# Two chained transformer networks: second network's attention in 12 steps of 512 columns, its preparation between projection chunks, and 8 modulation chunks moved into a feed-forward

## The reference, cut to what matters

```python
mod = (silu(c) @ w_ada[l] + b_ada[l])                 # six vectors of 1024: shift, scale, gate, twice
h = rmsnorm(x) * (1 + scale_a) + shift_a
proj = h @ w_in                                       # 1956 columns
o_f = dense_causal_attention(q_f, k_f, v_f, F)        # fox: 4 heads of 64, with a decay F
o_m = moba_attention(q_m, k_m, v_m, t5_table)         # moba: 4 heads of 64, with a bias table
q_lat = rmsnorm(c_q) @ w_uq;  kv = rmsnorm(c_kv) @ w_ukv
o_c = dense_causal_attention([q_nope, rope(q_rot)], [k_nope, rope(k_r)], v_c)   # mla: 8 heads of 96
y = concat(rmsnorm(o_f), rmsnorm(o_m), rmsnorm(o_c)) @ w_out
x = x + gate_a * rmsnorm(y)
x = x + gate_f * rmsnorm(swiglu(rmsnorm(x) * (1 + scale_f) + shift_f))          # hidden width 2816
```

## Time and profile before

| | us |
|---|---|
| median of 3 runs (2060.04 to 2062.87) | 2060.85 |
| time of the profiled execution | 2062.21 |
| its span | 2060.4 |
| PE busy | 1817.9 (88%) |
| DVE busy | 1160.3 (56%) |
| ACT busy | 691.5 (34%) |
| mean granted clock of TensorE | 0.901 |

### The profile page before, as it was taken

How to read it: one execution, slowest core, us unless ns; L and a number is a source line. 1 busy time by engine, 2 the same in 40 slices (tenths; PEclk the granted TensorE clock), 3 DMA queues, 4 the chain that set the end, 5 groups by cost and what they waited for, 6 DMA issues and landing times.

```text
span 2060.4 us, 25840 instructions
## 1 busy us (share of the span) xinstructions
PE 1817.9 (88%) x10564; PEld 1460.7 (71%) x10564; DVE 1160.3 (56%) x1915; ACT 691.5 (34%) x883; POOL 116.5 (6%) x97
## 2 busy tenths in 40 slices
PE   5998987989999998979789979885999798859997
PEld 2775654768888887746579967444999684649996
DVE  2475455564454455654667664558665645486654
ACT  2423333241312223433343433342443233424431
POOL 1010002010000001100100000003000000030000
PEclk7998767999999999978899989887999999579999
DMA  8324455122322322344345536761564458215642
GB/s 317 122 83 164 164 205 184 41 103 82 110 94 82 121 66 95 130 164 164 113 167 181 204 131 227 273 239 50 176 198 162 154 213 298 70 49 177 198 163 89
DMA packets 172086, 310.26 MB, mean 151 GB/s; under 512 B 3232, under 2 KB 60576, under 8 KB 171328
## 3 DMA queue, kind: packets, MB, share of 16 engines
q1 hardware_dynamic: 168304, 295.03, 41.3%
q10 hardware_dynamic: 3376, 12.01, 1.7%
q0 software_dynamic: 288, 1.57, 0.2%
HBM read 306.50 MB, written 2.10 MB: 150 GB/s over the span
## 4 chain that ended last, share of the span: by engine, by line
PE 70%; DVE 17%; issue 5%; ACT 5%; DMA 2%; POOL 1%; DVEq 0%; ACTq 0%; SPq 0%; POOLq 0%
PE bank L503 52%; PE twin L503 14%; DVE arena L1059 4%; PE bank L512 4%; DVE ring_r L1059 3%; ACT arena L1689 2%; ACT arena_r L1689 2%; DMA ring<-in_w_mod 1%; DVE arena L1624 1%; DVE arena_r L1059 1%; POOL rs L1982 1%; DVE params L1059 1%; DMA ring<-in_w_in 1%; DVE params L1489 1%; DVE arena L1139 1%
## 5 line engine op out<-in xcount | busy, mean ns | idle before, releaser
L503 PE MATMUL bank<-arena_r 128*128 128x512 f32 (+2 forms) x2016 | 665.5, 374 | 4.7 <-DVE params L1505 4.4
L1059 DVE TENSOR_TENSOR ring_r<-ring,arena_r 128x4096 fp32r<-128x4096 f32 (+5 forms) x90 | 380.2, 4225 | 242.2 <-ACT arena_r L1689 242.1
L503 PEld LDWEIGHTS bank<-arena_r 128*128 128x128 f32 x2016 | 385.1, 191 | 74.1 <-DVE params L1505 5.1
L1689 ACT ACTIVATE arena_r<-ring 128x4096 fp32r<-128x4096 f32 (+5 forms) x92 | 322.6, 3507 | 339.4 <-PE bank L503 294.0
L503 PE MATMUL bank<-arena_r,actT_r 128*128 128x512 f32 (+5 forms) x768 | 267.5, 388 | 27.8 <-DVE ring_r L1059 17.4
L1689 ACT ACTIVATE arena<-bank 128x256 f32<-128x256 f32 (+6 forms) x236 | 109.0, 462 | 521.9 <-PE bank L503 411.9
L503 PE MATMUL twin<-actT_r,arena_r 128*128 128x256 f32 x1408 | 255.2, 284 | 0.5 <-DVE actT_r L1059 0.4
L503 PEld LDWEIGHTS twin<-actT_r,arena_r 128*128 128x128 f32 x1408 | 220.6, 193 | 1.0 <-DVE actT_r L1059 0.9
L503 PE MATMUL bank<-ring_r,arena_r 128*128 128x512 f32 x560 | 219.2, 391 | 0.0
L503 PE MATMUL bank<-ring_r,actT_r 128*128 128x512 f32 (+5 forms) x576 | 216.0, 375 | 0.0
L503 PE MATMUL twin<-actT_r,ring_r 128*128 128x256 f32 x704 | 199.6, 284 | 0.0
(11 more groups left out here) (165 smaller groups left out, 1804.4 us busy)
## 6 DMA issues: line engine op xcount, KB each, us to landing
ring<-in_w_mod SPq DMA_DIRECT2D x24, 2048.0 KB, 8.2
ring<-in_w_ada SPq DMA_DIRECT2D x24, 2048.0 KB, 8.0
ring<-in_w_gate_up SPq DMA_DIRECT2D x44, 1024.0 KB, 7.4
ring<-in_w_down SPq DMA_DIRECT2D x20, 2048.0 KB, 7.9
ring<-in_w_up SPq DMA_DIRECT2D x16, 2048.0 KB, 7.8
ring<-in_w_out SPq DMA_DIRECT2D x8, 2048.0 KB, 8.1
ring<-in_w_down SPq DMA_DIRECT2D x8, 1792.0 KB, 7.5
ring<-in_w_in SPq DMA_DIRECT2D x6, 2048.0 KB, 8.9
```

What stands on the lines that cost most here:

```text
L503: ins = nc.tensor.matmul(out_, lhsT, rhs, start=start, stop=stop)
L1059: return v.tensor_tensor(o, x, y, op)
L1689: return nc.scalar.activation(o, x, func, **kw)
```

## The change

1. Attention of the second network goes in 12 steps (`STEPS2`) that fill a 512-column bank: four heads of the first query tile, or two heads of the second. Scores of step j are issued beside the transposes of j-2 and the values of j-4 (`AHEAD = 4`). The values have a column of ones, so that the sum of the weights comes with them and ACT no longer accumulates.
2. The columns of `w_in_2` are reordered on the host, so that the latent columns come first. Preparation stands between the chunks: chunk 0 and 1, latent norms, chunk 2, transposes and latent products, first scores, chunk 3.
3. Group norms of fox and moba are done inside the loop, and `out2` half 0 starts with their half of the rows, before the mla norm is ready. The split of `out2` chunk 0 is wholly DVE's and stands at step 8.
4. Batch 2 of modulation (8 chunks) is multiplied in the feed-forward of layer 0 of the first network, one chunk before each first and one after each second down chunk. Batch 3 moves to the mixer of layer 1 of the first network (8 of its 12) and the second network's layer 0 (4). Its layer 1 still has 8.
5. The list of loads follows: `par2` before chunk 3 of `in2`, one modulation chunk between the halves of `out2`.

```diff
+BESIDE1 = [16, 8]
+BESIDE2 = [4, 8]
+UP_FILLS = [8, 0]
+        for q in range(4):
+            m = UP_FILLS[l] // 8
+            out += [("up1", l, 2 * q + i) for i in range(2)] + take(m)
+            out += [("down1", l, 2 * q)] + take(m) + [("down1", l, 2 * q + 1)]
+    for l in range(L):
+        ins = [("in2", l, c) for c in range(len(CH2))]
+        out += ins[:3] + [("par2", l, 0)] + ins[3:] + take(BESIDE2[l] - 1)
+        out += [("out2", l, 0)] + take(1) + [("out2", l, 1)]
+        out += [("up2", l, c) for c in range(F2 // 256)]
...
-    if key[0] == "out2" and key[2] == 0:
-        return 0
...
+STEPS2 = [(kind, part[0], part[1]) for kind in ("fox", "moba")
+          for part in (((0, 1, 2, 3), 0), ((0, 1), 1), ((2, 3), 1))]
+STEPS2 += [("mla", (0, 1, 2, 3), 0), ("mla", (4, 5, 6, 7), 0)] + [("mla", (h, h + 1), 1) for h in (0, 2, 4, 6)]
+AHEAD = 4
...
# PE, layer1, feed-forward of layer 0
+                    if l == 0:
+                        fill()
                     for half in range(2):
                         w = weights(("down1", l, 2 * q + half))
...
+                    if l == 0:
+                        fill()
...
# PE, layer2
+                for j in range(AHEAD, len(STEPS2) + AHEAD):
+                    values(j - AHEAD)
+                    if j - 2 < len(STEPS2):
+                        weights_turned(j - 2)
+                    if j < len(STEPS2):
+                        scores(j)
                         fill()
+                    if j == AHEAD:
+                        pe.wait_ge(heads_ready, nth(heads_ready))
+                        done("a", mark["kv", l])
+                    if j in (AHEAD, AHEAD + 1):
+                        for hp in (2 * (j - AHEAD), 2 * (j - AHEAD) + 1):
+                            for src, r in ((ql, "v"), (kc, "a")):
+                                turned_heads(lambda t, h: src[:, t, 96 * h:96 * h + 96], "mla", 96, hp, r)
+                    if j == 11:
+                        pe.wait_ge(mixt_ready, nth(mixt_ready))
+                        for pr in range(2):
+                            mixed_turned(0, pr, "v")
...
# DVE, layer2
+                    if j == 8:
+                        split([("out2", l, 0)])
+                    if j == 9:
+                        for at, t, c0, c1 in two:
+                            squares(sq2[:, 0:c1 - c0], mix2[:, t, c0:c1], at)
...
+                    if j == 10:
+                        group_scales(two)
```

More of the change, by code:

```diff
@@ L430, in _ @@
                         sp.wait_ge(x_ready, updates(kind, l))
+                    if kind == "par2":
+                        first = PLACE["in2", l, 0]
+                        sp.wait_ge(slot_read, sum(x not in MODS for x in order[:first + 1]))
                     w, n = (a["par1"], p1n) if kind == "par1" else (a["par2"], p2n)
@@ new lines, in layer2 @@
+                scores(0)
+                scores(1)
+                done("v", mark["in2", l, 2, 0])
+                done("a", mark["in2", l, 2, 1])
+                for hp in range(2):
+                    for at, r in ((0, "v"), (256, "a")):
+                        turned_heads(lambda t, h: qkm[:, t, at + 64 * h:at + 64 * h + 64], "moba", 64, hp, r)
+                fill()
+                project(3, 0)
+                weights_turned(0)
+                weights_turned(1)
+                scores(2)
@@ new lines, in layer2 @@
+                done("v", mark["mix2", l, 0, 1])
+                gate(L + l, 2, 0, 0)
+                w = weights(("out2", l, 0))
+                banks = [take("v") for t in range(TS)]
+                for t, (b, filled) in enumerate(banks):
+                    for i in range(4):
+                        three(b[:, :], mixed(t)(i), [x[:, i, :] for x in w], i == 0, False)
+                pe.wait_ge(mixt_ready, nth(mixt_ready))
+                for pr in range(2):
+                    mixed_turned(1, pr, "a")
@@ new lines, in layer2 @@
+                done("a", mark["mix2", l, 1, 1])
+                for t, (b, filled) in enumerate(banks):
+                    for i in range(4, KT):
+                        three(b[:, :], mixed(t)(i), [x[:, i, :] for x in w], False, i == KT - 1,
+                              filled if i == KT - 1 else None)
+                gate(L + l, 2, 0, 1)
+                w = weights(("out2", l, 1))
+                for t in range(TS):
+                    b, filled = take("v")
+                    linear(b[:, :], mixed(t), lambda i: [x[:, i, :] for x in w], filled)
@@ L1569, in layer2 @@
+                two = [(0, 0, 0, 256), (1, 1, 0, 256), (2, 0, 256, 512), (3, 1, 256, 512)]
+                third = [(4, 0, 512, 1024), (5, 1, 512, 1024)]
+                for hp in range(2):
+                    turned_heads(qfT, 66, hp)
                 for t in range(TS):
@@ new lines, in layer2 @@
+                at, t, c0, c1 = third[1]
+                squares(sq2[:, 0:c1 - c0], mix2[:, t, c0:c1], at)
+                v.tensor_scalar(ms[:, 4:6], ss[:, 4:6], 1.0 / 512, EPS, ALU.mult, ALU.add).then_inc(ms_ready, 1)
+                handed.append(("power", 4, 2))
+                group_scales(third)
+                for pr in range(2):
+                    dve.wait_ge(a_filled, mark["mix2", l, 1, pr])
+                    b = AB[(mark["mix2", l, 1, pr] - 1) % 2]
+                    rest2(1, pr, b).then_inc(a_emptied, 1)
@@ L1939, in layer2 @@
-                act.wait_ge(v_filled, mark["pv2", l])
-                split([("out2", l, 0)])
-                turned_mix((1, 3, 5, 7), S, act2_lo)
-                nth(s_filled, len(UNITS2))
-                for half in range(2):
-                    split(after(("out2", l, half)))
+                    turned_heads(kmT, 64, hp)
+                exponents2(1)
+                weights_turned(0)
+                weights_turned(1)
+                exponents2(2)
+                b = filled()
+                step(f(vfm[:, 1, :, 0:64], b[:, :].rearrange("p (h c) -> p h c", c=64), ACT.Copy), a_emptied)
@@ L1945, in layer2 @@
+                split(after(("out2", l, 0)))
+                for pr in range(2):
+                    b = filled()
+                    step(f(mix_hi2[1][:, 2 * pr:2 * pr + 2, :], b[:, :].rearrange("p (a n) -> p a n", a=2), ACT.Copy),
+                         mixh_ready)
+                split(after(("out2", l, 1)))
+                nth(s_filled, len(STEPS2))
+                nth(a_emptied, 2)
                 normed([0, 1], 2 * (L + l) + 1)
```

554 lines of the change are left out of this document (304 added, 250 removed).

## The result

The changed kernel takes 2130.5 us (2125.2 to 2131.8), the kernel before beside it 2060.4; the ratio is 1.0333 with an interval of 1.0313 to 1.0352. It is slower by 70 us. The prediction said slower, with 2097 and a range of 2060 to 2122: the direction was right, the size was not, and the time lies outside the range.

The account below looks back on a forecast made before the run. PE, busy 88% of the span, was taken as either full of products or waiting on other engines. Feed-forward +70, layer 0 -20, layer 1 -13.5 gave +36.5 on 2062.2, so 2098.7, put at 2097 for the median; range 2060 to 2122.

Parts of the forecast that it names:

- Part 1: First network's layer 0 feed-forward: modulation fills and late loads behind DVE's split cost +70 us (55 to 76).
- 4 x 9.5 + 3 x 5.85: Same feed-forward: PE stalls before tile 2, +9.5 us in four down a chunks and +5.85 in three down b chunks.
- 0.4 for the last: Last down b chunk of that feed-forward: only about 0.4 us, since the next chunk is a smaller `in1` chunk.
- down b lands at 11.3 to 11.6 after the start of down a: Feed-forward: down b's load follows B's, which has a 2 us start; PE's tile 2 then starts +9.5 us later.
- The bound of 12.1: Feed-forward: upper bound on down b's landing after down a starts, giving 10.2 us of stall each (+41).
- Sum of the feed-forward: 14.4 + 38 + 17.5 + 0.4 = +70: Layer 0 feed-forward: seven fills 14.4, down a stalls 38, three down b stalls 17.5, the last 0.4 us.
- Part 2: Behind the second network's output projection: `up2` chunk 0 loads later, +8 us per layer (5 to 9).
- Parts 3 and 4: Second network: mixer's end -19 us per layer (12 to 22); preparation gains about nothing, sum 76.3 us before 74.9.
- Part 5: Second network's attention loop: loads set its end, at 138 in layer 0 (-9 us) and 143 in layer 1 (-2.5).
- the feed-forward hides the loads: Rival for the feed-forward: loads still arrive in time and only fills cost, -19 us overall, 2042; chance 0.08.
- attention gains its full room: Rival for the second network: loops keep full clock, ending at 122 and 130, -62 us; 2054 to 2069; chance 0.15.
- its loops do not shorten: Rival for the second network: late loads and half clock hold loops at 146 to 152, giving 2114; chance 0.17.

Follow-up runs that it names:

- out2_order: Changed kernel with all modulation loads of each second-network layer put ahead of its two `out2` loads: 2112.8 us.
- loop_products_alone: Changed kernel without the eight modulation loads of the second network's layer 1, their products kept on a constant: 2110.0 us.
- early_mod: Changed kernel with one modulation load of each second-network layer put ahead of the last projection chunk's load: 2115.4 us.
- late_split: Changed kernel with DVE's split of the next chunk put behind tile 1's take-out in layer 0 feed-forward down chunks: 2052.0 us.
- late_out2_par: Changed kernel with DVE's split behind tile 1's take-out, modulation loads ahead of both `out2` loads, and `par2` ahead of the third projection chunk's load: 2045.9 us.

## Why the prediction was right in direction and wrong in size

**Part 1, the stall: the mechanism right, the size low.** Each down chunk has the wait before tile 2, released by DVE, for the reason given; moving the split removed it. The sum had 4 x 9.5 + 3 x 5.85 = 55.6 us and 0.4 for the last; the waits have 64.8 in 8 times: 11.6, 11.3, 10.5 and 10.4 in the down a chunks, 6.2, 7.8 and 6.3 in the first three down b chunks, and 0.8 in the last. The 7.8 follows an up chunk's load that took 9.4 us and not 7.8. The step that was mis-sized is "down b lands at 11.3 to 11.6 after the start of down a". It gave load B a start of 2 us; in the trace it is issued at 474.08 and down b at 474.99, a start of 0.9, and down b landed after 13.7, 13.4, 12.6 and 12.5. The bound of 12.1 was too low as well; 13.6, the row I had for two loads issued together, should have been the upper end.

**Part 1, the missing term: the clock.** "Sum of the feed-forward: 14.4 + 38 + 17.5 + 0.4 = +70" has no term for what a stall does to the products behind it. It was 20.1 us. The prediction's own rows had shown that level in attention, and it priced the attention's steps with it, but not the feed-forward. There I counted on full clock since the earlier trace rows had it; but those rows are of a round without a stall. This term is the larger part of the miss: of 97.9 - 70 = 28, 20 are clock, 7.6 the longer idle time (63.2 against 55.6), and the fills at 14.6 against 14.4 were right.

**Part 2, +8 per layer: right.** The wait of 7.78 and the split behind it ended 16.4 us after half 0 was read. The order in out2_order took it away.

**Parts 3 and 4: nearly right.** The end of the mixer in layer 0, 34.8 before, is 18.65 us (1477.63 to 1496.28), predicted 16; in layer 1 it is 17.9 (1875.21 to 1893.12). Preparation starts the loop as said: the load of the third modulation chunk is issued 76.1 and 75.8 us after the projection's start (76.3).

**Part 5: right in kind.** The loop ends at 141.2 and 142.3, predicted 138 and 143 (147.4 and 145.5 before). That the loads set this end is shown for layer 1 by loop_products_alone; for layer 0 only early_mod's 5.6 us speak for it. Layer 0 gained 14.2 (20 predicted), layer 1 12.6 (13.5).

**The rivals.** That the feed-forward hides the loads was false, and late_split shows what it takes to make it true: the rival named a landing within 2 us of the chunk's start as the point of decision, while the order of two DVE instructions decided with landings unchanged. That attention gains its full room, and that its loops do not shorten, were both false; the layers lie between. No case had the feed-forward above 76, so no case reached 2130.

## What to carry to other kernels

A split or prefetch step that waits for a load should stand behind the take-outs that PE needs next, not ahead of them; then a late load costs nothing until its own first use (late_split: the same late loads, and PE idle for 7.4 us as in the kernel before). When a ring is given more loads, price each stall twice: the wait itself and the products after it at half clock (here 63 and 20 us), and take the landing of a load behind another in the queue from the row of two together. Work that is moved from a stage bound by its loads to one bound by PE pays only after that first point is seen to, so the parts of such a change are best timed one by one.

## What the runs showed of the hardware

POOL's power of four values took 1.02 us in the earlier trace rows and 5.12 us in the changed kernel, where it starts beside DVE's split (timeline of layer 0):

```profile
1356.56 4.42 DVE L1137 TENSOR_TENSOR ring_r<-ring,arena_r 128x4096 fp32r<-128x4096 f32 x1
...
1356.73 5.12 POOL L2164 TENSOR_TENSOR rs<-ms,neghalf 128x4 f32<-128x4 f32 x1 [18.42 <-DVE ms L1619]
...
1361.96 1.78 DVE L1628 SCALAR_TENSOR_TENSOR arena<-arena,rs,params 128x256 f32<-128x256 f32 x4 [0.78 <-POOL rs L2164]
```

It ends 0.87 us after DVE does. In late_out2_par the split comes later, and the same power is alone:

```profile
1275.71 1.02 POOL L2169 TENSOR_TENSOR rs<-ms,neghalf 128x4 f32<-128x4 f32 x1 [18.66 <-DVE ms L1624]
```

The Trainium skill (SBUF — State Buffer, "SBUF: two separate sides") says that a DVE operation with two SBUF inputs and a GpSimd operation that reads SBUF exclude each other for the whole instruction, whichever starts first. The rows agree. The scalings that need the power stand behind the split in DVE's own order and waited 0.78 us for it, so it cost at most about that here; no run moved the power alone.

In the feed-forward of the changed kernel the second of two 2 MB loads issued 0.9 us apart landed 12.5 to 13.7 us after its issue; the up chunks' loads in the chain, with no other ahead of them, took 7.82, 9.44 and 7.88.
